# Two more modulation units summed by VectorE between the takes of a down sweep

## The reference, cut to what matters

```python
def modulation(cond, w_mod, b_mod):
    m = jax.nn.silu(cond) @ w_mod + b_mod
    return jnp.split(m[..., None, :], 6, axis=-1)
...
shift1, scale1, gate1, shift2, scale2, gate2 = modulation(cond, p['w_mod'], p['b_mod'])
h = rmsnorm(x, p['g_mix']) * (1 + scale1) + shift1
...
h2 = rmsnorm(x, p['g_ffn']) * (1 + scale2) + shift2
u = h2 @ p['w_up'] + p['b_up']
...
x = x + gate2 * ((jax.nn.silu(gg) * a) @ p['w_down'])
```

## Time and profile before

| | |
|---|---|
| median of 3 runs | 2311.07 us (2310.56 to 2314.61) |
| the profiled execution | 2310.93 us |
| its span, first to last instruction | 2309.1 us |
| TensorE busy / VectorE / ScalarE / GpSimd | 99% / 58% / 40% / 33% |
| granted TensorE clock | 0.999 of full speed |
| the four sweeps of group 0 | about 841.7 to 899.6 us of the span |
| the last sweeps' part of group 1 | (1,0,1) from about 1027.4, (1,1,1) until 1070.3 |

### The profile page before, as it was taken

How to read it: one execution, slowest core, us unless ns; L and a number is a source line. 1 busy time by engine, 2 the same in 40 slices (tenths; PEclk the granted TensorE clock), 3 DMA queues, 4 the chain that set the end, 5 groups by cost and what they waited for, 6 DMA issues and landing times.

```text
span 2309.1 us, 40205 instructions
## 1 busy us (share of the span) xinstructions
PE 2278.8 (99%) x16886; PEld 2051.5 (89%) x16886; DVE 1328.3 (58%) x2304; ACT 927.3 (40%) x1765; POOL 752.7 (33%) x498
## 2 busy tenths in 40 slices
PE   7999999999999999999999999999999999999998
PEld 6887898888989998998988879888899899899897
DVE  5456458644436766766663573785443467547456
ACT  3345346633335331331363452555442443223223
POOL 0331322111333544544422303220123335444442
PEclk9999999999999999999999999999999999999999
DMA  9313222223232324223242143222232322222211
GB/s 330 128 58 122 77 94 81 78 77 122 97 114 74 92 92 128 74 92 123 78 142 72 39 134 100 78 67 92 74 111 94 110 81 74 84 66 81 81 60 69
DMA packets 221905, 221.60 MB, mean 96 GB/s; under 512 B 10582, under 2 KB 191390, under 8 KB 221470
## 3 DMA queue, kind: packets, MB, share of 16 engines
q1 hardware_dynamic: 212999, 193.77, 26.2%
q10 hardware_dynamic: 8727, 25.27, 3.2%
HBM read 209.90 MB, written 9.11 MB: 95 GB/s over the span
## 4 chain that ended last, share of the span: by engine, by line
PE 93%; DVE 3%; ACT 3%; issue 1%; POOL 1%; DMA 0%; SPq 0%; POOLq 0%; DVEq 0%; ACTq 0%
PE ps L905 51%; PE ps L1056 12%; PE ps L1593 11%; PE ps L1515 4%; PE ps L1195 3%; PE ps L1212 2%; PE ps L925 1%; PE ps L1156 1%; PE ps L1171 1%; PE ps L1021 1%; PE ps L1141 1%; PE ps L1177 1%; PE ps L1417 1%; PE ps L916 1%; POOL w_lo L864 1%
## 5 line engine op out<-in xcount | busy, mean ns | idle before, releaser
L864 POOL TENSOR_TENSOR w_lo<-raw,w_hi 128x512 fp32r<-128x512 f32 (+1 forms) x486 | 742.5, 1558 | 1534.4 <-ACT w_hi L1665 981.2
L905 PE MATMUL ps<-h_hi,w_hi 128*128 128x320 f32 (+2 forms) x2368 | 615.1, 312 | 0.0
L905 PE MATMUL ps<-h_hi,w_lo 128*128 128x320 f32 (+2 forms) x2368 | 607.1, 309 | 0.0
L905 PE MATMUL ps<-h_lo,w_hi 128*128 128x320 f32 (+2 forms) x2368 | 606.7, 309 | 0.0
L905 PEld LDWEIGHTS ps<-h_hi,w_hi 128*128 128x128 f32 x2368 | 413.2, 188 | 7.1 <-issue 4.6
L905 PEld LDWEIGHTS ps<-h_lo,w_hi 128*128 128x128 f32 x2368 | 413.2, 188 | 0.2
L905 PEld LDWEIGHTS ps<-h_hi,w_lo 128*128 128x128 f32 x2368 | 413.1, 188 | 0.0
L1665 ACT ACTIVATE w_hi<-raw 128x2048 fp32r<-128x2048 f32 (+2 forms) x110 | 203.8, 1852 | 272.9 <-PE ps L1593 120.8
L2701 DVE TENSOR_SCALAR conv<-u_pad,vcol 128x642 f32<-128x642 f32 x88 | 90.1, 1024 | 149.6 <-ACT u_pad L2102 148.0
L1593 PE MATMUL ps<-w_hi,a_hi 128*128 128x512 f32 x440 | 172.4, 392 | 0.6 <-POOL w_lo L864 0.6
L1593 PE MATMUL ps<-w_lo,a_hi 128*128 128x512 f32 x440 | 171.4, 390 | 0.0
(11 more groups left out here) (358 smaller groups left out, 3517.6 us busy)
## 6 DMA issues: line engine op xcount, KB each, us to landing
raw<-in_w_mod SPq DMA_DIRECT2D x44, 1024.0 KB, 5.0
raw<-in_w_up SPq DMA_DIRECT2D x88, 512.0 KB, 4.7
raw<-in_w_gate SPq DMA_DIRECT2D x32, 1024.0 KB, 5.3
raw<-in_w_in SPq DMA_DIRECT2D x16, 1024.0 KB, 5.0
raw<-in_w_down SPq DMA_DIRECT2D x16, 1024.0 KB, 4.9
w_br<-in_w_branch ACTq DMA_DIRECT2D x8, 1024.0 KB, 4.8
raw<-in_w_out SPq DMA_DIRECT2D x8, 1024.0 KB, 4.9
raw<-in_w_down SPq DMA_DIRECT2D x8, 768.0 KB, 4.4
```

Source lines behind the costliest of these rows:

```text
L864: ins = nc.gpsimd.tensor_tensor(w_lo[part_slot(li, s)][:, c0:c1], raw[HOME[u]][:, c0:c1], w_hi[part_slot(li, s)][:, c0:c1].bitcast(F32), A ...
L905: ins = mm(out, w_at(w_hl[wi]), at_(x_hl[xi]), start=first and q == 0, stop=final and q == 2)
```

## The change

Units 1 and 5 join `SUMMED`. Their sums are made in four pieces of four instructions, each piece ahead of the take of one of the tiles 0 to 3 of the sweep (g, 0, 1). TensorE's `mod_rows` for them becomes `mod_sums`, and the buffer of M1 and M5 is released by the last of VectorE's sixteen instructions and not by TensorE's product.

```diff
-SUMMED = (2, 3, 6, 7)
+SUMMED = (1, 2, 3, 5, 6, 7)
...
-                def sum_ahead(n):
+                def sum_ahead(n, first=0, end=2 * KD, added=[]):
 
                     u = UNIT_AT[li + 1, "mod", MOD_ORDER[n]]
-                    ve.wait_ge(raw_loaded[HOME[u]].sem, loaded_count(u))
+                    if first == 0:
+                        added.clear()
+                        ve.wait_ge(raw_loaded[HOME[u]].sem, loaded_count(u))
                     w = raw[HOME[u]][:, 0:2048].rearrange("p (k n) -> p k n", k=KD)
-                    added = []
                     for k in range(KD):
                         for v in range(2):
+                            if not first <= 2 * k + v < end:
+                                continue
                             out, by = mod_sum[:, n % 2, v, :], cond_c[:, k, 2 + v:3 + v]
...
                     if kh and (g, dh) != (len(UP_GROUPS) - 1, 1):
                         for t in range(T):
+                            if li + 1 < DEPTH and i in PAIR_AT and dh == 0 and t < 4:
+                                sum_ahead(PAIR_AT[i], 4 * t, 4 * t + 4)
                             take_down(g, dh, t)
```

## The result

The changed kernel takes **2317.89 us** in the median of 11 runs (2316.78 to 2319.31), the kernel before in the same comparison 2312.37 (2310.55 to 2315.13, 11 runs). The ratio is **1.0022 [1.0014, 1.003]**: 5.5 us slower. That is inside the whole range of the forecast, 2309.3 to 2319.0, but above the forecast's own range (2311 to 2316.3), more than twice the +2.6 of the sum, and above the 2315.7 up to which it was called no change; the interval of the ratio lies on both sides of that 0.2%. The profiled executions say the same: 2316.80 against 2310.93, spans of 2315.0 against 2309.1, +5.9.

A forecast was written before the change was run, and what follows sets the result against it. TensorE was taken as the bound, its matmuls without gaps. The profiled 2310.93 us plus 2.6 (+1.4 in group 0, +1.2 in group 1, the saving of 1.34 already counted) gave 2313.5 us, range 2309.3 to 2319.0.

The forecast's parts named there:

- What bounds the kernel: Over down sweeps of groups 0 and 1 matmuls follow without a gap; TensorE is busy 99% of the span.
- what TensorE saves: At the sweep transitions of units 1 and 5: 0.67 us each, together -1.34 us, if nothing is late.
- What VectorE gets: 16 instructions per unit, about 1.6 us per piece in 1.3 us idle; without GpSimd, 1.8 us to spare.
- What it collides with: VectorE's sums meet GpSimd's `w_lo` of D(0,1,0) and D(1,1,0), whose slacks are 1.8 and 0.85 us.
- a run of sums already going holds GpSimd back: VectorE against GpSimd: GpSimd waits for the run's next gap; a sum finding GpSimd going waits, then they alternate.
- The sum: Late last sums delay D(0,1,0) by 1.4 us and D(1,1,0) by 1.2 us, saving already counted: +2.6 us.
- GpSimd 0.4 us later relative to it: Group 1, sweep before D(1,1,0): GpSimd comes 0.4 us later relative to take 1 than in group 0; +1.2 us.
- What hangs on the lateness: D(0,1,1)'s load and `w_lo` come later: 0.2 us to spare, 0.1 in group 1; nothing added, no slack left.
- Rival 1: At both transitions the pieces fit and the last sum is there by 870.5: -1.34 us, 2309.6, or part; 17%.
- Rival 2: At D(0,1,1), M3's sums hold GpSimd's fourth quarter; TensorE waits 5.3 us: 2318.8 once, 2324.1 in both groups; 20%.
- Rival 3: At units 1 and 5 the change does not replace `mod_rows`; under 1%.
- The number: Whole kernel: 2313.5 us, own range 2311 to 2316.3; 62%, with slower by over 0.2% at 21%.

The follow-up runs named there:

- low_short: The changed kernel with GpSimd's four instructions on D(0,1,0) and D(1,1,0) cut from 512 columns to 16 each; 2311.31 us, 0.9989 of the kernel before.
- all_first: The changed kernel with all sixteen sums of a unit ahead of the take of tile 0; 2311.68 us, 0.9995 of the kernel before.
- eights: The changed kernel with the sums in two pieces of eight, ahead of the takes of tiles 0 and 1; 2311.35 us, 0.9992 of the kernel before.
- rows_kept: The changed kernel, sums of units 1 and 5 made but unused, TensorE computing these units from their rows; 2315.4 us, 1.001 of the kernel before.
- change_again: The changed kernel itself, unedited, measured again in a second comparison; 2318.96 us, 1.0023 of the kernel before.

## Why the prediction was right, and where it was off

- **What bounds the kernel; what TensorE saves.** Right. Wherever the sum came in time (low_short, all_first, eights) the gap is 0.68, and their profiles show 0.67 us gained at each transition.
- **What VectorE gets.** Right: pieces of four take 1.67 to 1.79 us when nothing meets them, and in low_short the last sum ends at 872.33, 1.8 us ahead of the 874.16 at which TensorE wants it: the number counted.
- **What it collides with.** Right in the cause, wrong in the order. The rule that a run of sums already going holds GpSimd back did not apply to the third piece: GpSimd entered at 863.95 after one sum. The three others then took turns with it, and the fourth piece, which the text had alternating, met nothing. Last sum at 871.87 where 872.5 was written. The rule of the Trainium skill that was weighed against it ("SBUF — State Buffer", "Who interferes with whom": the pair of ports belongs to whoever issued first, for the whole instruction) had GpSimd enter after each sum of the third piece. This trace bears that out there: 1.51 us for each of the last three sums beside quarters of 1.47. It doesn't elsewhere in the same trace (879.00, below).
- **The sum.** Group 0 +1.1 for +1.4, group 1 +1.9 for +1.2, together +3.0 for +2.6. Group 1 was mis-sized by the step "GpSimd 0.4 us later relative to it". That was read from one execution, in which the load in group 1 was slow (7.90 us from issue to first quarter against 7.48 in group 0). In the changed kernel it took 7.01, GpSimd was 0.4 us earlier relative to the sweep than in group 0, and all four sums met it. A range of 6.9 to 7.9 us for this time would have given waits of 1.7 or 2.4 us in either group.
- **What hangs on the lateness.** Right, and by a count of tenths. GpSimd's first quarter of D(0,1,1) was held:

```profile
879.00 3.33 POOL L864 TENSOR_TENSOR w_lo<-raw,w_hi 128x512 fp32r<-128x512 f32 x1 [9.39 <-ACT w_hi L1665]
...
879.00 7.36 POOL L864 TENSOR_TENSOR w_lo<-raw,w_hi 128x512 fp32r<-128x512 f32 x4 [9.39 <-ACT w_hi L1665]
```

  Done at 886.36, wanted at 886.56: 0.2 us of slack, the number that was forecast, and no wait. rows_kept, where TensorE came earlier, is over that edge.
- **Rival 1** (the pieces fit) fell: 16 sums did not pass beside GpSimd in pieces of four, though they did in eights. **Rival 2** (5.3 us in one go) did not happen. **Rival 3** fell: 16 records at L955 instead of 64 at L925.
- **The number.** The direction and the cause of the wait were right; that the measured 2317.9 us lies in the range is in part luck. It is above the forecast's own 2316.3, and the range reached to 2319.0 only for rival 2, which did not happen. The term that failed is one that isn't in the sum: a wait was priced at its own length. Behind it TensorE ran at the 1.2 GHz level for 3.41 us in the profile, and over all runs the change has 1.2 such stretches more than before, about 2 us. The two gaps cost 3.0 us in the one profile and 3.8 in change_again (with some of the half clock in it), and with about 2 of clock that is near the +5.5 and +5.8 of the medians. The chance for "slower by over 0.2%" had the wrong owner: it was given to a late `w_lo`, and what brought the time over that edge was the clock and the longer wait.

## What to carry to other kernels

Work that is put into an engine's idle time must be placed against the engines that share its memory ports, not only against its own free time: the same 16 sums per unit cost TensorE 3.0 us over both groups when cut into fours, and saved it 1.3 when cut into eights, because the fours reached further into GpSimd's stretch. Don't take the arrival of the other engine from one execution: here a load and its rounding took 6.9 to 7.9 us, and that alone made the wait 1.7 or 2.4 us. And a new wait of TensorE can cost more than its length: look at the granted clock behind it, in many runs, and compare their mean clocks before giving the rest of a difference to the work.

## What the hardware showed that was not expected

- **When a run of sums holds GpSimd.** Held: 879.00 (3.33 us for a quarter that takes 1.28 alone), 1051.31 (3.21), 887.51 before. Not held: 863.95, after one sum; and 1037.70 in eights, where GpSimd comes during the sixth sum of a run and the seventh waits (1.52 us). In group 0 of eights it comes with the seventh and gets in before the last, which waits (1.39). What decides it the runs don't show.
- **The price of turns is not shared.** Taking turns, a sum of 0.48 us becomes 1.51, a quarter of 1.28 becomes 1.47. Here the engine with the short instructions pays nearly all.
- **Half-clock stretches in busy work.** The changed kernel's at 1580 us stands at L1074 and L1417, where twenty matmuls of 128x2 go ahead of larger ones, with no idle time of TensorE in its 8 us (8.00 busy). It lasts 3.41 us, as the one behind the wait does. In the thirteen profiles the clock falls at this place, which comes once in each layer, 8 times in 26.
